# Five norms of a two-part transformer block: first two panels interleaved by operand chunk, third panel in buffers of its own, constant products on TensorE around the norms

## What is computed

```python
def rms_norm(x, g):
    xf = x.astype(jnp.float32)
    y = xf * lax.rsqrt(jnp.mean(xf * xf, axis=-1, keepdims=True) + EPS)
    return (y * g.astype(jnp.float32)).astype(x.dtype)
...
        xn = rms_norm(x, g_norm1[l]) * (1 + scale1) + shift1
        p = xn @ w_in[l]
...
    xn = rms_norm(x, g2) * (1 + scale2) + shift2
    return x + gate2 * swiglu(xn, w_fi, w_fo)
...
    for layer in range(DEPTH):
        u = rms_norm_2(h, pre_norm[layer])
        if layer % 2 == 0:
            e = layer // 2
            y = even_layer(u, positions, even_w_in[e], even_conv_w[e], even_conv_b[e], ret_gn[e], even_w_out[e])
        else:
            o = layer // 2
            y = odd_layer(u, positions, odd_w_in[o], q_a_norm[o], w_qb[o], kv_a_norm[o], w_kvb[o], odd_w_out[o])
        h = h + rms_norm_2(y, post_norm[layer])
```

## Time and profile before

| | us |
|---|---|
| three runs | 2347.71, 2350.8, 2354.86 |
| median | 2350.8 |
| the profiled execution, its own time | 2349.86 |
| its span, first to last instruction | 2347.7 |

### The profile page before, as it was taken

The page is one execution under the profiler, slowest core; times in us unless marked ns, Lnnn a source line. Parts: engine busy times, 40 slices in busy tenths (PEclk is TensorE's granted clock), DMA queues, the critical chain, the costliest instruction groups (busy, mean ns, idle before and its releaser), DMA issues.

```text
span 2347.7 us, 26539 instructions
## 1 busy us (share of the span) xinstructions
PE 2205.1 (94%) x10994; PEld 1775.6 (76%) x10994; DVE 1216.9 (52%) x1580; ACT 726.0 (31%) x1057; POOL 649.6 (28%) x283
## 2 busy tenths in 40 slices
PE   5898897999999999799989999989999999899997
PEld 5785576888888888685668888867788888777665
DVE  5995676566556665686444213256231443511455
ACT  2323524222112221424532212222272222244532
POOL 2100002223332233200144444433234444233202
PEclk9999998999999999899999999999999999799998
DMA  7312142334333332211023323323223333221201
GB/s 260 121 46 90 37 148 68 108 126 139 104 108 126 126 125 100 67 54 72 28 77 99 117 72 99 114 66 95 76 64 94 95 99 99 63 72 52 79 1 54
DMA packets 60167, 213.59 MB, mean 91 GB/s; under 512 B 6672, under 2 KB 10384, under 8 KB 59792
## 3 DMA queue, kind: packets, MB, share of 16 engines
q1 hardware_dynamic: 57888, 206.92, 27.5%
q10 hardware_dynamic: 2160, 4.98, 0.6%
HBM read 209.77 MB, written 2.10 MB: 90 GB/s over the span
## 4 chain that ended last, share of the span: by engine, by line
PE 86%; DVE 8%; ACT 3%; issue 2%; DMA 1%; POOL 1%; SPq 0%; ACTq 0%; DVEq 0%
PE prod L548 73%; PE misc L586 2%; PE prod L712 1%; PE misc L648 1%; DMA ring<-in_wmod 1%; PE prod L680 1%; DVE operand_lo L1405 1%; PE prod L599 1%; PE prod L767 1%; ACT operand_hi L1036 1%; PE misc L896 1%; PE misc L791 1%; PE prod L967 1%; DVE work L1433 1%; PE misc L779 1%
## 5 line engine op out<-in xcount | busy, mean ns | idle before, releaser
L527 POOL TENSOR_TENSOR wlo<-ring,whi 128x1024 fp32r<-128x1024 f32 (+3 forms) x256 | 608.1, 2376 | 1608.4 <-ACT whi L983 1608.4
L548 PE MATMUL prod<-operand_hi,whi 128*128 128x512 f32 (+1 forms) x2208 | 734.4, 373 | 35.7 <-DVE operand_lo L1421 14.1
L548 PE MATMUL prod<-operand_hi,wlo 128*128 128x512 f32 (+1 forms) x2208 | 721.7, 367 | 0.0
L548 PE MATMUL prod<-operand_lo,whi 128*128 128x512 f32 (+1 forms) x2208 | 719.8, 366 | 0.0
L983 ACT ACTIVATE whi<-ring 128x1024 fp32r<-128x1024 f32 (+3 forms) x284 | 293.4, 1034 | 737.2 <-PE prod L548 737.2
L548 PEld LDWEIGHTS prod<-operand_hi,whi 128*128 128x128 f32 x2208 | 380.8, 190 | 124.9 <-issue 28.2
L548 PEld LDWEIGHTS prod<-operand_hi,wlo 128*128 128x128 f32 x2208 | 379.8, 190 | 68.7
L548 PEld LDWEIGHTS prod<-operand_lo,whi 128*128 128x128 f32 x2208 | 379.7, 190 | 68.5 <-issue 2.4
L1471 DVE CUSTOM_DVE_ANT_0 mod_junk<-modw,silu_c,par 128x1024 bf16<-128x1024 f32 x68 | 127.8, 1880 | 78.9 <-DMA modw<-in_wmod 78.3
L548 PE MATMUL prod<-hidden_hi,whi 128*128 128x512 f32 (+1 forms) x528 | 160.6, 358 | 0.0
L548 PE MATMUL prod<-hidden_hi,wlo 128*128 128x512 f32 (+1 forms) x528 | 160.4, 358 | 0.0
(11 more groups left out here) (244 smaller groups left out, 2224.2 us busy)
## 6 DMA issues: line engine op xcount, KB each, us to landing
ring<-in_w SPq DMA_DIRECT2D x224, 512.0 KB, 3.6
modw<-in_wmod SPq DMA_DIRECT2D x68, 512.0 KB, 3.7
ring<-in_w SPq DMA_DIRECT2D x32, 704.0 KB, 4.9
ring<-in_wmod SPq DMA_DIRECT2D x28, 512.0 KB, 5.2
dft<-in_dftx SPq DMA_DIRECT2D x8, 512.0 KB, 5.7
resid<-in_xt SPq DMA_DIRECT2D x1, 3072.0 KB, 13.9
ring<-in_w SPq DMA_DIRECT2D x12, 192.0 KB, 2.3
ret_r<-in_decay ACTq DMA_DIRECT2D x8, 256.0 KB, 3.0
```

Of the source, the lines that this page charges most:

```text
L527: nc.gpsimd.tensor_tensor(wlo[j % 2][:, 0:w], ring[PLACE["panel", j] % RING][:, 0:w], whi[j % 2][:, 0:w].bitcast(F32), ALU.subtract).then_ ...
L548: mm = pe.matmul(G[b][:, t0:t0 + tn], w[v][:, k * P:(k + 1) * P], a[:, t0:t0 + tn], start=(i == 0 and q == 0), stop=(i == g.kc - 1 and q = ...
```

## The change

Three parts, in five products (`TWO_FIRST`) and at seven norms.

1. In `big()`, for a product in `TWO_FIRST`, TensorE takes chunk i for panel 0 and then chunk i - 2 for panel 1, so that both run along with the operand. What followed panel 0 and panel 1 (`after`) follows both.
2. The third panel of these products has buffers `whi`/`wlo` of its own (`third`), in memory that is free at that time. Its high part moves on ScalarE from the end of panel 0 to behind the norm's root. GpSimd's order stays; its low part can start as soon as the high part is there. VectorE's low parts (`win1`) get one more wait that keeps the count of low parts in order.
3. `keep_busy(count)` issues products of the constant `ones` with 256 columns of the constants, in float32, into the PSUM tile `M1`, which nobody reads. At the norms whose squares are summed beforehand (`total`) 4 stand ahead of the column sums; at all seven after the first norm 3 stand between the sums and the transposes, and 4 (512 tokens) or 7 (768 tokens) behind these.

```diff
+TWO_FIRST = ("fin00", "win1", "fin10", "eqk", "oin")
+THIRD = {GEMM[name].j0 + 2: name for name in TWO_FIRST}
...
+        third = {}
+        for name, hi_at, lo_at in (("fin00", 9 * NT, 14 * NT), ("win1", NT, 3 * NT), ("eqk", 16 * NX, 18 * NX), ("oin", 0, 13 * NX)):
+            third[name] = [at(f"{which}_{name}", DC * P, F32R, region + 4 * o) for which, o in (("whi", hi_at), ("wlo", lo_at))]
+        third["fin10"] = third["fin00"]
+
+        def whi_of(j):
+            return third[THIRD[j]][0] if j in THIRD else whi[j % 2]
...
                     for q, (w, a) in enumerate(((whi_of(j), high(k)), (whi_of(j), low(k)), (wlo_of(j), high(k)))):
...
-                for p in range(begin, g.n if panels is None else panels):
+                two = name in TWO_FIRST
+                for i in range(g.kc + 2 if two else 0):
+
+                    for p in range(2):
+                        if 0 <= i - 2 * p < g.kc:
+                            panel(name, p, high, low, width(p) if callable(width) else width, i - 2 * p, i - 2 * p + 1, ready=first_ready)
+                for p in range(2 if two and after is not None else 0):
+                    after(p)
+                for p in range(2 if two else begin, g.n if panels is None else panels):
...
+            def keep_busy(count):
+
+                for _ in range(count):
+                    pe.matmul(M1[:, 0:256], ones, con[:, 0:256], start=True, stop=True)
+
...
             def rms(nchunks, width, sq_tiles, by_head=False, free=None, total=None):
+
+                first = n["rope"] == 0
+                wait(pe, rope_done, n["rope"])
+                wait(pe, ret_copied, 8 if n["rope"] > 8 else 0)
+                keep_busy(4 if total is not None and not first else 0)
                 sum_squares(nchunks, width, sq_tiles, by_head, total)
+                keep_busy(0 if first else 3)
                 spread_roots(width, sq_tiles, free)
+                keep_busy(0 if first else 4 if width == NX else 7)
...
-                        high(j + 2)
+                        if j + 2 not in THIRD:
+                            high(j + 2)
...
+                else:
+                    high(GEMM[("win", "fin")[which] + str(l) + "0" * which].j0 + 2)
...
             root(NX, 1024)
+            high(GEMM["eqk"].j0 + 2)
             normed_high(XH, DC, W)
...
             root(NX, 1024)
+            high(GEMM["oin"].j0 + 2)
             normed_high(XH, DC, W)
...
+                dve.wait_ge(lo_ready, j)
                 dve.wait_ge(hi_ready, j + 1)
```

More of the change, by code:

```diff
@@ L369, in build_program, with wlo_of @@
         assert max(endA, endB) <= SBUF_END - 10 * DC * P and endD <= SBUF_END - 8 * DC * P
+        third = {}
[4 more added lines that the diff above has]
+            return third[THIRD[j]][0] if j in THIRD else whi[j % 2]
+        def wlo_of(j):
+            return third[THIRD[j]][1] if j in THIRD else wlo[j % 2]
         def ps(name, width):
@@ L526, in _ @@
                     pool.wait_ge(hi_ready, j + 1)
-                    nc.gpsimd.tensor_tensor(wlo[j % 2][:, 0:w], ring[PLACE["panel", j] % RING][:, 0:w],
-                                            whi[j % 2][:, 0:w].bitcast(F32), ALU.subtract).then_inc(lo_ready, 1)
+                    nc.gpsimd.tensor_tensor(wlo_of(j)[:, 0:w], ring[PLACE["panel", j] % RING][:, 0:w],
+                                            whi_of(j)[:, 0:w].bitcast(F32), ALU.subtract).then_inc(lo_ready, 1)
         @block.tensor
@@ L537, in panel @@
                 j = g.j0 + p
-                b, v = BANK[j], j % 2
+                b = BANK[j]
                 if first == 0:
@@ L545, in panel @@
                         ready(k)
-                    for q, (w, a) in enumerate(((whi, high(k)), (whi, low(k)), (wlo, high(k)))):
+                    for q, (w, a) in enumerate(((whi_of(j), high(k)), (whi_of(j), low(k)), (wlo_of(j), high(k)))):
                         for t0, tn in [s for s in SEGS if s[0] < width]:
-                            mm = pe.matmul(G[b][:, t0:t0 + tn], w[v][:, k * P:(k + 1) * P], a[:, t0:t0 + tn],
+                            mm = pe.matmul(G[b][:, t0:t0 + tn], w[:, k * P:(k + 1) * P], a[:, t0:t0 + tn],
                                            start=(i == 0 and q == 0), stop=(i == g.kc - 1 and q == 2))
@@ L982, in high @@
                     landed(act, ("panel", j))
-                    nc.scalar.activation(whi[j % 2][:, 0:w], ring[PLACE["panel", j] % RING][:, 0:w], ACT.Copy).then_inc(hi_ready, 1)
+                    nc.scalar.activation(whi_of(j)[:, 0:w], ring[PLACE["panel", j] % RING][:, 0:w], ACT.Copy).then_inc(hi_ready, 1)
             def stage(name, evac=None, after=None, norm_follows=False, panels=None):
@@ L1393, in panel_low @@
                 w = KC_OF[j] * P
+                dve.wait_ge(lo_ready, j)
                 dve.wait_ge(hi_ready, j + 1)
-                nc.vector.tensor_tensor(wlo[j % 2][:, 0:w], ring[PLACE["panel", j] % RING][:, 0:w], whi[j % 2][:, 0:w].bitcast(F32),
+                nc.vector.tensor_tensor(wlo_of(j)[:, 0:w], ring[PLACE["panel", j] % RING][:, 0:w], whi_of(j)[:, 0:w].bitcast(F32),
                                         ALU.subtract).then_inc(lo_ready, 1)
```

## The result

| | before | changed |
|---|---|---|
| median of 11 runs each | 2354.2 | 2344.3 |
| lowest, highest | 2347.7, 2363.8 | 2330.7, 2348.0 |
| the profiled execution, its own time | 2349.86 | 2342.06 |
| its span | 2347.7 | 2340.3 |
| its mean granted clock | 0.976 | 0.983 |

The ratio is 0.9948 (95% interval 0.9928 to 0.9967): the kernel became faster by 12.2 us, between 7.8 and 17, of the median before (the two medians alone differ by 9.9). The forecast was 19.3, and 2331.5 for the time. So the sign was right, the size was not, and the time lies outside the range given (2323 to 2341).

The account below looks back on a forecast made before the run. TensorE, busy 94% of the span, was taken as the bound. Gains of 16.6 (paired panels), 0 (buffers) and 2.7 (fillers) made 19.3 off 2349.9, so 2330.6, plus 0.9 for the median: 2331.5 us; range 2323 to 2341.

Parts of the forecast that it names:

- What bounds the kernel: Whole kernel: TensorE, busy 94% of the span, bounds it; gains only where it waits or runs slowly, in and behind norms.
- Part 1, 16.6 us: First two panels of five products: fewer pieces behind the last chunk remove 4.6, 3.4, 3.0, 2.8 and 2.8 us of wait.
- provided that the clock is full from the start: At `fin10`: condition on the 3.0 us gain, that TensorE has full clock from the pair's start.
- Part 2, 0 by itself: Third panel's own buffers: no gain alone, but keep panel 2 from being late when it starts 3 to 5 us earlier.
- Part 3, 3.4 - 0.7 = 2.7: Fillers at the norms: faster column sums and transposes gain 3.4 us, fillers outlasting idle time lose 0.7, net 2.7.
- about 0.1 lost at each of seven norms: Three fillers between sums and transposes take 1.5 us against 1.38 or 1.20 idle plus some 0.1 pipeline; 0.7 in all.
- All of it is wait that goes: Paired panels: no product is added or dropped, so the whole 16.6 us is removed wait.
- Rival 1: Some norms: clock falls all the same, losing 2 to 3.5 us per 768-token norm, 2 at `oin`; 2338 us, chance 0.12.
- rival 3: Behind the paired panels: third panel's low part or fourth panel late, wait only moves; 2342 to 2347, 2344 taken, chance 0.06.
- Rival 2: Plain norms: VectorE and GpSimd collide in full, each loses 2.34 us, 4.7 in all; 2336 us, chance 0.03.
- What would show it: Signs, right: `win1` panel 1 ends about 3 us after chunk 7's first product; wrong: 0.8 us fillers between sums and transposes.
- at the next norm: Sign for wrong: time gained at one norm is missing again at the next norm.

Follow-up runs that it names:

- r4: Changed kernel without the third panel's own buffers (it waits in `whi[0]`): median 2348.5 us, ratio 0.9978 to the kernel before.
- r2: Changed kernel without any constant products (fillers): median 2342.9 us, ratio 0.9952 to the kernel before.
- r7: Changed kernel without the three constant products between column sums and transposes: median 2335.7 us, ratio 0.9908 to the kernel before.
- r11: Changed kernel with chunk i taken for both panels at once and no constant products: median 2342.4 us, ratio 0.995 to the kernel before.
- r12: Changed kernel, both panels at once, no middle fillers, one 128-column filler behind each chunk's sums in `oin`'s second norm: 2335.9 us, ratio 0.9919 to the kernel before.

## Why the prediction was off, point by point

- **What bounds the kernel**: right. TensorE's waits and its clock in the norms were the places to gain, and all the gain came from there.
- **Part 1, 16.6 us**: nearly right. From the first chunk's product to the fourth panel's copy, means of the profiles, `win1` gained 3.3 (forecast 3.4), `fin00` 4.35 (4.6), `eqk` 2.8 (2.8), `oin` 2.85 (2.8) and `fin10` 1.7 (3.0). Sum 15.1. The one that is short is the one given "provided that the clock is full from the start": it was at the start, but in three of five it fell behind the first chunks, to 0.66 between 1197 and 1202 in the first, and the pair took 13.8 us there instead of 12.5.
- **Part 2, 0 by itself**: right, and so was the 2 us a norm that it keeps away (r4).
- **Part 3, 3.4 - 0.7 = 2.7**: in the norms 17.25 - 15.1 = 2.15. The gain of 1.2 at `fin00`'s sums came, though r2 has it without fillers too. The price of the three middle fillers, "about 0.1 lost at each of seven norms", was mis-sized. Held against r7 it is 1.5 at `oin` alone, where they take 0.97 each, up to 0.4 at `fin00`, and nothing at the three others of the five.
- **The step that failed** is in the sum. "All of it is wait that goes", 19.3 off the profiled execution, takes for granted that the other 2090 us stay as they were. They lengthened by 4.9 in the mean (from 291.8 to between 290.6 and 300.0), by low clock in stretches that the change never touched. The sum had no term for that, which puts it at nothing without a reason. What the profiles show is that the kernels with an edit at the norms lose more there (14 of 15 profiles). That the shorter norms bring it about is not shown. Rival 1, the clock falling all the same, was priced for the norms only (2338), and rival 3 looked for a wait, not for a clock. Rival 2 did not come: VectorE's low parts at `eqk` and `oin` took 0.68 to 0.70 in all five profiles. Of the 7 us between 19.3 and 12.3, 4.9 are this, 1.5 part 1 (1.3 of it at `fin10`) and 0.55 part 3.
- **The base**: 3.4 us of the miss in the absolute time are not of the change. The three runs shown had a median of 2350.8; 72 runs of that kernel, all experiments together, have one of 2355.2. The profiled execution was near the lowest of them, partly since `fin00` ran in its faster pattern in it, and in none of the three others. The range took 3 us for scatter, where single executions of one kernel spread over 15 and more. The measured time is 12.8 above the forecast: 3.4 of the base, the 7 above, and 2.4 by which the two medians differ less than the mean spans of the profiles, which is scatter.
- **"What would show it"**: the signs named as right came (3.1 us in `win1`, fewer waits for odd chunks, panel 2 without a wait longer than before), but for two: full clock through `fin10`, and transposes within 0.2 of VectorE, which at `oin` waited for the fillers. Two of the signs for wrong came. Fillers of 0.8 us and more stood between sums and transposes at `oin` (0.97 each). And gained time was missing again, though not "at the next norm": the mixers' stretch begins some 80 us behind `win1`'s first panels, the one in `ogate` some 30 us behind those of `oin`, the one in `oout` 105 us later.

What stays open is why the clock falls in `ogate` and ahead of `oout` in some executions: the rows show that it does, not what sets it off. Fewer or longer gaps between the products of the attention were not tried.

## What to carry to other kernels

Cut the span into stretches by marks that both kernels have, and compare every stretch, also those that the change doesn't touch, in several profiled executions of each: a median alone could not have told that 17 us were gained and 5 lost. In a kernel near full clock, a forecast that adds up removed waits needs a term for the clock elsewhere, and its base should be more than one execution. When work can start as operands arrive, try to do all of it at once rather than staggered: here that gained 4 to 12 us more, but nothing in the norms without the constant products around them (r11 against r2). And free the buffer that it needs next: 9 us of this change hung on two spare buffers.

## What the runs showed of the hardware

**Two patterns for the same matmuls.** In `fin00`, 768 tokens are a product of 512 columns and one of 256, by turns, at a granted clock of 1.00 and with no wait. In the kernel before's first profile such pairs start 0.347 us apart:

```profile
499.98 0.51 PE L548 MATMUL prod<-operand_hi,whi 128*128 128x512 f32 x2
...
501.02 0.51 PE L548 MATMUL prod<-operand_hi,whi 128*128 128x512 f32 x2
```

and in the second profile of the changed kernel 0.353:

```profile
500.55 0.51 PE L564 MATMUL prod<-operand_hi,whi 128*128 128x512 f32 x2
...
501.61 0.51 PE L564 MATMUL prod<-operand_hi,whi 128*128 128x512 f32 x2
```

Three pairs take 1.04 there and 1.06 here. Whichever pattern `fin00` settles in after its first panels it keeps to its end, 16 panels later, for 133.1 or 135.7 us; the same program showed both. The same shapes in `fin01` ran at 0.353 in every profile. With the 256 columns first (r8) it was 0.353 again in both:

```profile
620.33 0.52 PE L564 MATMUL prod<-hidden_hi,whi 128*128 128x256 f32 x2
...
621.38 0.52 PE L564 MATMUL prod<-hidden_hi,whi 128*128 128x256 f32 x2
```

1.05 for three pairs. So the order doesn't move it, and what does is open. It is 2.6 us of the scatter between executions, which no edit of a norm explains. The Trainium skill, TensorE: Matmul & The Clock Gate, section Back-to-back issue gap, gives N / 2.4 + 2.5 ns for the isolated gap of a matmul with N columns at full clock, and 131 ns for each of a sustained stream with 512 columns. Worked out from the formula, this pair would take an estimated 325 ns. Neither agrees with the rows here, in which the pair takes 347 or 353, and the 0.69 us of a chunk in `win1` gives 230 for each product of 512 columns; the measurement decides.

**A filler is not a warm clock.** Constant products took 0.51 us each at 2.4 GHz and 0.97 at 1.2. At `fin10` they kept the clock up in two of five profiles through the pair; in the 64 one-column sums ahead of `oin` they never did to the end: the clock was full for the first sums and then fell, in r12 too, where TensorE was busy without a gap. What was forecast as either full clock or none is one more thing that differs between executions.
